# A three-block model on one core: the up products of the feed-forward stages by seven half-size products per pair of weight tiles

## The reference

```python
def sq_relu_mlp(h, w_up, w_down):          # first block, both layers, width 4096
    return jnp.square(jax.nn.relu(h @ w_up)) @ w_down
```

## Time and profile before

| | |
|---|---|
| median of 3 runs | 2861.84 us (2861.54 to 2865.23) |
| span of the profiled execution | 2860.9 us |
| TensorE busy | 98% of the span, granted clock 0.993 in the mean |
| VectorE, ScalarE, GpSimd busy | 52%, 35%, 48% |
| HBM | 94 GB/s over the span |

### The profile page before, as it was taken

The page is one execution under the profiler, slowest core; times in us unless marked ns, Lnnn a source line. Parts: engine busy times, 40 slices in busy tenths (PEclk is TensorE's granted clock), DMA queues, the critical chain, the costliest instruction groups (busy, mean ns, idle before and its releaser), DMA issues.

```text
span 2860.9 us, 43560 instructions
## 1 busy us (share of the span) xinstructions
PE 2799.9 (98%) x17428; PEld 2463.7 (86%) x17428; DVE 1479.0 (52%) x2439; ACT 1000.0 (35%) x1489; POOL 1376.9 (48%) x1748
## 2 busy tenths in 40 slices
PE   9989999999999999999899999999999999999999
PEld 7768888877788888998799999999989799999887
DVE  8955322267532227897644544233798745444241
ACT  4453222255422224443353322223443345322221
POOL 6426554555654556542225555456542225555554
PEclk9999999999999999999999999999999999999999
DMA  5103322222232224223324222222322243332322
GB/s 187 60 25 103 102 96 89 97 97 79 96 96 92 96 99 126 98 74 98 85 83 142 88 89 92 94 85 93 113 81 78 65 118 116 98 102 89 102 90 74
DMA packets 122630, 270.79 MB, mean 95 GB/s; under 512 B 22864, under 2 KB 57040, under 8 KB 122192
## 3 DMA queue, kind: packets, MB, share of 16 engines
q1 hardware_dynamic: 73104, 245.98, 26.0%
q10 hardware_dynamic: 49344, 22.19, 2.8%
HBM read 249.52 MB, written 18.61 MB: 94 GB/s over the span
## 4 chain that ended last, share of the span: by engine, by line
PE 42%; issue 29%; POOL 24%; DVE 4%; POOLq 0%; ACT 0%; DMA 0%; ACTq 0%; DVEq 0%
PE acc L666 33%; POOL w_lo L638 24%; PE acc L1078 2%; PE acc L1059 2%; PE aux L1059 2%; PE aux L1092 1%; DVE index_score L2706 1%; DVE best L2699 1%; PE acc L1286 0%; PE aux L969 0%; PE acc L1092 0%; PE acc L920 0%; PE aux L1278 0%; PE aux L951 0%; PE acc L1148 0%
## 5 line engine op out<-in xcount | busy, mean ns | idle before, releaser
L638 POOL TENSOR_TENSOR w_lo<-w_raw,w_hi 128x256 fp32r<-128x256 f32 x1744 | 1376.7, 821 | 1467.8 <-ACT w_hi L1320 1467.0
L666 PE MATMUL acc<-n_hi,w_hi 128*128 128x264 f32 (+1 forms) x2824 | 756.9, 323 | 2.3 <-DVE index_k L2398 1.3
L666 PE MATMUL acc<-n_lo,w_hi 128*128 128x264 f32 (+1 forms) x2824 | 748.0, 320 | 0.0
L666 PE MATMUL acc<-n_hi,w_lo 128*128 128x264 f32 (+1 forms) x2824 | 746.0, 319 | 0.0
L1320 ACT ACTIVATE w_hi<-w_raw 128x1024 fp32r<-128x1024 f32 (+1 forms) x436 | 454.1, 1043 | 615.2 <-PE acc L666 561.5
L666 PEld LDWEIGHTS acc<-n_hi,w_hi 128*128 128x128 f32 x2824 | 470.4, 188 | 59.8 <-issue 15.0
L666 PEld LDWEIGHTS acc<-n_lo,w_hi 128*128 128x128 f32 x2824 | 467.3, 188 | 40.9 <-issue 2.6
L666 PEld LDWEIGHTS acc<-n_hi,w_lo 128*128 128x128 f32 x2824 | 467.2, 188 | 38.3
L2214 DVE TENSOR_TENSOR x<-x,acc 128x512 f32<-128x512 f32 (+1 forms) x144 | 99.7, 692 | 562.6 <-PE acc L666 519.3
L666 PE MATMUL acc<-hidden_lo,w_hi 128*128 128x512 f32 (+1 forms) x1040 | 343.3, 358 | 0.0
L666 PE MATMUL acc<-hidden_hi,w_lo 128*128 128x512 f32 (+1 forms) x1040 | 342.7, 357 | 0.0
(11 more groups left out here) (484 smaller groups left out, 3750.0 us busy)
## 6 DMA issues: line engine op xcount, KB each, us to landing
w_raw<-in_stream SPq DMA_DIRECT2D x420, 512.0 KB, 3.5
unit_blocks<-unit_scratch ACTq DMA_DIRECT2D x26, 256.0 KB, 4.0
w_raw<-in_stream SPq DMA_DIRECT2D x16, 384.0 KB, 3.0
unit_scratch<-unit_staged ACTq DMA_DIRECT2D x20, 256.0 KB, 2.8
saved_x<-x SPq DMA_DIRECT2D x2, 2112.0 KB, 10.5
x<-saved_x SPq DMA_DIRECT2D x16, 264.0 KB, 2.7
saved_gates<-root ACTq DMA_DIRECT2D x12, 264.0 KB, 2.1
unit_scratch<-unit_staged ACTq DMA_DIRECT2D x1, 2560.0 KB, 13.4
```

Of the source, the lines that this page charges most:

```text
L638: i = pool.tensor_tensor(wl[:, slot, s], raw[:, slot, s], wh[:, slot, s].bitcast(F32), ALU.subtract)
L666: last = pe.matmul(o, w[:, p % W_SLOTS, P * b:P * b + P], r, start=(b == 0 and i == 0), stop=(b == n - 1 and i == 2))
```

## The change

The four feed-forward stages are reordered. The hidden tiles are cut into chunks of 4 (in a layer 3, 3, 4, 4, 4, 4). The first chunk is computed as before ("whole"). From then on a "pair" of pieces (in an mlp stage two up tiles, in a layer the gate and the value tile) is a 2x2 matrix of halves: two tiles by rows 0 to 511 and 512 to 1023, against the tokens' 2x2 matrix of row halves by token halves (256 or 264 tokens). Its eight half-size products are replaced by seven (Strassen's scheme in Winograd's form), named a11, s1, a12, s2, s4, s3, a22 in the order in which they run. Each is four blocks by three matmuls of 256 or 264 columns, into banks of `aux`. s1, s2, s4, s3 use sums of weight halves, which DVE makes from `w_raw` (s3 in place in `w_raw`), and sums of the normed tokens, made once per stage before the second whole tile is taken out. ACT copies three intermediate products out of PSUM (`keep_product`), DVE adds them to others (`pair_product`).

Pieces are split by half pieces ("ops"): the ring now has eight halves, and ACT and POOL split each of the seven factors (512 columns each) instead of the two pieces. Down pieces hold two output tiles of a chunk of 4. After a pair's first six products come the down pieces that are due (two in an mlp stage, one in a layer with chunks of 4), each of two ops, and only then a22. `freed` tells SP when a slot of `w_raw` may be loaded again: for the first piece of a pair when s3 has been split, for the second when a22 has. POOL's loop becomes straight code.

Per mlp stage there are 4 whole pieces, 14 pairs and 64 down ops; per layer 6 whole pieces, 19 pairs and 48 down ops. The cut diff:

```diff
+MLP_CHUNKS = [(n, n + 4) for n in range(0, FF // P, 4)]
+FFN_CHUNKS = [(0, 3), (3, 6)] + [(n, n + 4) for n in range(6, FT2, 4)]
+
+
+def chunks_of(stage):
+    return MLP_CHUNKS if stage.startswith("mlp") else FFN_CHUNKS
+
+
+def feed_steps(stage):
+
+    chunks, gated = chunks_of(stage), stage.startswith("layer")
+    order = [("whole", 0, n) for n in range((2 if gated else 1) * chunks[0][1])]
+    for e in range(1, len(chunks)):
+        n = (chunks[e][1] - chunks[e][0]) // (1 if gated else 2)
+        for i in range(n):
+            order.append(("pair", e, i))
+            order += [("down", e - 1, k) for k in range(4 * i // n, 4 * (i + 1) // n)]
+    return order + [("down", len(chunks) - 1, k) for k in range(4)]
...
+FACTORS = ("a11", "s1", "a12", "s2", "s4", "s3", "a22")
+SUMS = ("s1", "s2", "s4", "s3")
+LATER = 2
...
+    def freed(self, p):
+
+        found = [n + 1 for n, (kind, piece, _) in enumerate(self.ops) if piece == p or (piece == p - 1 and kind == "a22")]
+        paired = [n + 1 for n, (kind, piece, _) in enumerate(self.ops) if piece == p and kind == "s3"]
+        return paired[0] if paired else max(found)
...
-            sp.wait_ge(w_lo, p - RAW_SLOTS + 1)
+            sp.wait_ge(w_lo, order.freed(p - RAW_SLOTS))
...
-        with nc.Fori(0, pieces, W_SLOTS, engines=(mybir.EngineType.Pool,)) as p:
-            for slot in range(W_SLOTS):
-
-                pool.wait_ge(w_hi, p + slot + 1)
-                for part in range(4):
-                    s = slice(2 * P * part, 2 * P * part + 2 * P)
-                    i = pool.tensor_tensor(wl[:, slot, s], raw[:, slot, s], wh[:, slot, s].bitcast(F32), ALU.subtract)
-                i.then_inc(w_lo, 1)
-
+        for o, (kind, p, part) in enumerate(order.ops):
+            slot, at = order.half(o)
+            n = width_of(o)
+            source = weights_of(o)
+            pool.wait_ge(w_hi, o + 1)
+            for a in range(0, n, 2 * P):
+                z = min(a + 2 * P, n)
+                i = pool.tensor_tensor(wl[:, slot, at + a:at + z], source[:, a:z],
+                                       wh[:, slot, at + a:at + z].bitcast(F32), ALU.subtract)
+            i.then_inc(w_lo, 1)
...
+            def banded(o, bank, hi, lo, opens):
+
+                slot, at_ = order.half(o)
+                for b in range(KT // 2):
+                    for i, (w, v) in enumerate(((wh, hi), (wh, lo), (wl, hi))):
+                        mm = pe.matmul(aux[:, bank, 0:width], w[:, slot, at_ + P * b:at_ + P * b + P], v[:, b, :],
+                                       start=(opens and b == 0 and i == 0), stop=(b == KT // 2 - 1 and i == 2),
+                                       skip_group_check=True)
+                mm.then_inc(w_used, 1)
+
...
+                elif kind == "s2":
+                    if u == 0:
+                        pe.wait_ge(t_ready, sums + 2)
+                    pe.wait_ge(product_kept, kept + 3 * u + 1)
+                    banded(o, X_BANK[u % 2], th[:, 1, :, 0:width], tl[:, 1, :, 0:width], False)
...
+        def split_before(o):
+
+            while at["split"] < len(order.ops):
                 q = at["split"]
...
+                if order.turned[q] + (LATER if order.ops[q][0] in SUMS else 0) > o:
+                    return
+                split_one()
...
+            for o in feed["ops"][:-KT]:
+                kind, p, u = order.ops[o]
+                split_before(o)
+                if kind == "a11":
+                    pair, since = u, 0
+                if kind in ("a11", "s1", "s2"):
+                    keep_product(o, u, SEQ // 2)
+                if kind == "s1" and u:
+                    hidden_high(feed["whole"] + 2 * u - 1)
+                if kind == "down":
+                    since += 1
+                    if since == 2:
+                        hidden_high(feed["whole"] + 2 * pair)
...
+            if name == "s1":
+                for q in (p, p + 1):
+                    dve.wait_ge(landed[q % RAW_SLOTS], 16 * (q // RAW_SLOTS + 1))
+            if name != "s3" and at["split"][n]:
...
+            if name == "s1":
+                i = dve.tensor_tensor(s1, a21, a22, ALU.add)
+            elif name == "s2":
+                i = dve.tensor_tensor(s2, s1, a11, ALU.subtract)
+            elif name == "s4":
+                i = dve.tensor_tensor(s4, a12, s2, ALU.subtract)
+            else:
+                i = dve.tensor_tensor(a21, a21, a11, ALU.subtract)
+            i.then_inc(w_sum, c.made(w_sum))
+            at["sum"] = c.mine()
...
+            whole(0)
+            token_sums(stage, gains)
+            whole(1)
+            token_sum_low(stage, 0)
+            weight_sum_of(stage, 0, "s1")
+            token_sum_low(stage, 1)
+            weight_sum_of(stage, 0, "s2")
+            whole(2)
+            token_sum_low(stage, 2)
+            weight_sum_of(stage, 0, "s4")
+            token_sum_low(stage, 3)
+            weight_sum_of(stage, 0, "s3")
+            whole(3)
+            low()
+            if layer:
+                two_norms_ahead()
...
+                if kind == "a12":
+                    pair, since = u, 0
+                    pair_product(o, ub[:, 0, 0:width], Y_BANK, 0, width)
                     if waiting:
                         low()
...
+                elif kind == "s4":
+                    pair_product(o, ub[:, 0, width:SEQ], Z_BANK, 2, width)
+                    dve.wait_ge(*c.mine())
+                    scaled = step(dve.scalar_tensor_tensor(ub[:, 0, 0:SEQ], ub[:, 0, 0:SEQ], 0.0, scale[:, ROW], ALU.max, ALU.mult))
+                elif kind == "s3":
+                    pair_product(o, ub[:, 1, width:SEQ], X_BANK[u % 2], 1, width)
+                    half_out = c.mine()
+                    dve.wait_ge(*scaled)
+                    squared(feed["whole"] + 2 * u)
+                    weight_sum_of(stage, u + 1, "s1")
+                elif kind == "a22":
+                    dve.wait_ge(w_used, o + 1)
+                    dve.scalar_tensor_tensor(ub[:, 1, 0:width], aux[:, X_BANK[u % 2], 0:width], 0.0, scale[:, first],
+                                             ALU.max, ALU.mult).then_inc(pair_out, c.made(pair_out))
+                    lower = c.mine()
+                    dve.wait_ge(*half_out)
+                    upper = step(dve.scalar_tensor_tensor(ub[:, 1, width:SEQ], ub[:, 1, width:SEQ], 0.0, scale[:, second],
+                                                          ALU.max, ALU.mult))
+                    weight_sum_of(stage, u + 1, "s3")
+                    dve.wait_ge(*lower)
+                    dve.wait_ge(*upper)
+                    squared(feed["whole"] + 2 * u + 1)
+                    if u == feed["pairs"] - 1:
+                        low()
+                elif kind == "down":
+                    down(o, d, stage, SEQ)
+                    d, since = d + 1, since + 1
+                    if since == 1:
+                        weight_sum_of(stage, pair + 1, "s2")
+                    elif since == 2:
+                        weight_sum_of(stage, pair + 1, "s4")
+                        low()
...
+                elif kind == "s4":
+                    pair_product(o, ub[:, i % 2, HALF:T], Z_BANK, 2, HALF)
+                    dve.wait_ge(*c.mine())
+                    gate = step(dve.tensor_tensor(ub[:, i % 2, :], ub[:, i % 2, :], scale[:, :], ALU.mult))
+                    weight_sum_of(stage, u + 1, "s1")
+                    convolve(i, gate)
+                elif kind == "s3":
+                    pair_product(o, rt[:, HALF:T], X_BANK[u % 2], 1, HALF)
+                    half_out = c.mine()
+                    weight_sum_of(stage, u + 1, "s2")
+                elif kind == "a22":
...
+                    gated(i, rt[:, :], upper)
+                    weight_sum_of(stage, u + 1, "s3")
```

More of the change, by code:

```diff
@@ L1464, in mixer0 @@
                 job()
[L1465 removed]
+            act.wait_ge(mixer_landed, 16)
             slopes(0)
@@ new lines, in layer @@
+            whole = feed["whole"] // 2
+            for i in range(whole):
+                split_before(used(at["piece"]))
+                gate_silu(i)
+                if i == 1:
+                    token_sums_high(stage)
+                split_before(used(at["piece"] + 1))
+                at["piece"] += 2
+                hidden_high(i)
+            for o in feed["ops"][:-KT]:
+                kind, p, u = order.ops[o]
+                split_before(o)
+                if kind in ("a11", "s1", "s2"):
+                    keep_product(o, u, HALF)
+                if kind == "s1" and u:
+                    hidden_high(whole + u - 1)
+                if kind == "s3":
+                    gate_silu(whole + u)
@@ L1783, in by_head @@
+            hidden_high(whole + feed["pairs"] - 1)
+            c.next(pair_out, 4 * feed["pairs"])
+            at["piece"] = feed["end"]
+            if STAGES[-1] != stage:
+                last_downs(feed, T, lambda k: vec2_(l + 1, "norm_mix_2", k))
+            else:
```

(13 more changed lines are left out.)

756 lines of the change are left out of this document (525 added, 231 removed).

## The result

The changed kernel takes **2963.7 us** (median of 4 runs, 2963.4 to 2966.8) against 2861.7 before: ratio 1.0362, 95% interval 1.0348 to 1.0377. It is 102 us slower; 2962 was forecast.

The account below looks back on a forecast made before the run. TensorE was taken to bound the kernel before, POOL's pair cycles after the change. To 2861.8 us it added 65.2 (mlp), 12.7 (layer0) and 22.6 (layer1), together +100.5: 2962 us, range 2838 to 3015.

Parts of the forecast that it names:

- TensorE's saving and pace: In all four feed-forward stages, 256-column matmuls at 0.119 us each; net 80 us saved if TensorE stays the limit.
- The rival of the slow weight load: Narrow matmuls on TensorE paced by their weight load, 0.189 us each; about 3197 us; chance 0.02.
- The mlp loop: In mlp pair cycles, a loop outside TensorE from s1 to the next s1: 23.6 us against 22.2 before, +19.6 per stage.
- turns: POOL and DVE alternate at SBUF: each two-SBUF-input DVE instruction costs a working POOL 0.45 us; 3.8 per mlp cycle.
- landing: In mlp cycles, loading the next pair's second piece after a22's split, then DVE's sum, ACT's rounding and hand-overs: 5.0 us.
- the half: POOL's time to split half a piece, including a hand-over of about 0.04 us: 1.48 us.
- TensorE stays the bound: Rival for the pair cycles: POOL seldom disturbed, so the kernel gets faster; 2820 us, or 2841; chance 0.20.
- The layer's cycle: In the layers' pair cycles, POOL at 17.8 us exceeds TensorE's 16.2; 18.0 taken in layer0, 17.8 in layer1.
- second loop: In the layers, a chain from a22 through DVE, ACT and TensorE back to a22, as long as POOL's: 16.9 to 17.7 us.
- The late chains: Rival in the layers: DVE waits for s3's half before the convolution, cycle 17.9 to 19.6; 3027 us; chance 0.10.
- Starts and the chunk of three pairs: In the layers, 5 us per start; three-pair chunk 53.8 us on POOL, costing +0.9 in layer0 and +2.8 in layer1.
- mlp starts: At each mlp stage's start, ACT rounds s1, s2, s4, s3 late behind hidden tiles: 11.5 us per stage, bounds 0 and 15.

Follow-up runs that it names:

- number 1: Changed kernel with a22 placed behind the first down piece after its pair, not behind all of them, in all four stages: 2898.3 us, 1.0130.
- number 8: Changed kernel with a22 behind the first down piece, s2, s4, s3 rounded earlier at mlp starts, and a11's copy ahead of roundings in layers: 2887.1 us, 1.0102.
- number 10: Pairs in the mlp stages only, with a22 early and start sums rounded earlier; the layers' feed-forward networks as in the kernel before: 2851.0 us, 0.9964.
- number 7: Changed kernel; in layers ACT copies a11's product before the roundings and POOL makes only half of each factor's low part (rest stale): 2897.8 us, 1.0127.
- number 2: Changed kernel with four added DVE scratch instructions, two SBUF inputs each, per mlp pair ahead of the wait for the load: 3010.4 us, 1.0528.
- number 4: Changed kernel; at mlp starts ACT rounds s2 ahead of the third hidden tile and s4, s3 ahead of the fourth: 2960.6 us, 1.0356.
- number 5: Changed kernel; in the layers ACT copies a11's product out of PSUM before rounding s3 and two down halves: 2947.9 us, 1.0311.
- number 6: Changed kernel; in the layers POOL makes the low part of only the first 256 of each factor's 512 columns, others stale: 2902.1 us, 1.0151.

## Why the prediction was right, point by point

**TensorE's saving and pace: right.** 12 matmuls of 256 columns take 1.41 to 1.43 us (0.118 each; 0.119 forecast). In numbers 1, 8 and 10 the mlp cycle is 21.0 where 21.1 was worked out; number 7 shows 16.0 in layer0 and 15.8 in layer1 where it was 16.2 and 15.85. The rival of the slow weight load is out.

**The mlp loop: right in kind, 0.9 us a cycle too dear.** Forecast 14.8 (ten halves) + 3.8 (turns) + 5.0 (landing) = 23.6; measured 17.65 + 5.04 = 22.7. In the stretch shown POOL's 20 instructions follow each other every 0.695 us where nothing disturbs them, 13.9 in all; seven take about 1.2 and two about 1.0, which makes the other 3.7. The term that was mis-sized is the half, 1.48 us: it held a hand-over for each half, and in a run there is none, since ACT rounds ahead. That is 14 x 0.9 = 13 us per stage, of which 11 and 8 are left once the starts are counted; number 1 shows that the placing of a22 is the whole of the loss within the cycles.

**The turns: right in the pair cycles, wrong at the start of an mlp stage.** In the cycles they cost 3.7 us against 3.8 in mlp, and 0.38 each by number 2 against 0.45. At the start, six such instructions without a pause between them cost POOL 4.6 us, 0.77 each (number 4). The rival "TensorE stays the bound" fell with them in the layers: there turns are 17.3 - 18 x 0.695 = 4.8 us of a cycle (4.5 forecast), and without them POOL's 12.5 would be far under TensorE's 16.2. In mlp it took the landing and the turns together: with a22 early and all turns left in, TensorE is the bound again (number 1), and by the sum above the loop without its 3.7 us of turns would be 19.0, under TensorE's 21.0 too.

**The layer's cycle: right in kind, 0.6 too dear.** 18.0 and 17.8 forecast, 17.3 and 17.2 measured in the steady part, again by the hand-overs. The "second loop" over ACT and DVE that I gave as equally long is no bound there (number 5 shortened it and won 0.2 us); in pairs 4 to 7, where POOL has smaller halves, shortening it helps (number 5), and so does less work on POOL (number 6). The late chains (3027 us) did not come.

**Starts and the chunk of three pairs: wrong, and this is the step that failed.** The prediction said that in a layer "three pieces go per cycle, so the second piece's slot is freed [...] earlier, and the landing is hidden", and charged POOL alone for the chunk: 53.8 us. The third pair has two down pieces, so four pieces go in it, as in an mlp cycle, and the landing that I had found there stands open here too. The first three cycles took 69.9 us in layer0 and 68.5 in layer1, 16 and 15 more than the 53.8 charged, and the 5 us charged for a start do not cover that. By the prediction's own terms the three cycles would be 17.2, 17.2 and 19.5; measured were 25.4, 17.4 and 27.1 in layer0 and 23.8, 17.4 and 27.3 in layer1. So the landing in the third pair is 7.6 and 7.8 us of the miss, and the rest is the first cycle, that is the start. Number 1 takes 6.8 and 7.9 us of the three cycles away (the landing), and number 6, without that edit, 7.8 in layer0 (POOL's share, nearly all of it in the first two cycles). For layer0 the account against TensorE's own time (387.9 - 27.9 = 360.0) is: chunk of three pairs 21.4 us where 5.3 was forecast, the other 16 pairs 24 where 29 was, the first whole tiles 3.5 where 5 was, and some 4 for the end and the stretches at 1.2 GHz where 1 was: 53 in place of 40. What part of the first cycle's 25.4 us falls to DVE's token and weight sums, and what to ACT's order, was not separated.

**mlp starts: right in size, wrong in reason.** 11.5 us and 1.5 for the end were charged. In number 8, where all cycles are TensorE's own, mlp0 takes 353.4 us against 357.4 - 14 x 1.12 = 341.7: 11.7 for start and end together, after the 1.8 us that number 4 had won at the gap; in mlp1 it is 10.6. But ACT's order was given as the cause of the gap. Number 4 rounds s1 four us earlier and TensorE gets it 1.8 earlier: what holds it is POOL, kept out by DVE's run of two-input instructions, which the price of 0.45 a turn does not show.

**The sum** came out within 2 us of the median (104.1 between the profiled executions, 100.5 forecast) because the two errors have opposite signs: 19 us too much in mlp, 25 too little in the layers, -2 elsewhere. That they cancel is luck. Not luck are the sign of the change, the landing loop in mlp and POOL as the bound of the layers' steady cycle. The misses of the parts, 19 and 25 us, would each have stayed inside the range of 2838 to 3015.

## What to carry to other kernels

Where an operation is placed later to save a wait, ask which buffer it still holds, and who must load into it: here one product at the end of the order put 3.5 us of transfer and 1.5 us of chain into the loop of every mlp pair. That made the cycle 1.8 us longer than TensorE's own and cost 66 us in all by number 1, the layers' third pairs included, where the scheme saves 80 on TensorE. A ring with as many slots as a cycle uses pieces leaves slack only as far as a slot is freed early in the cycle: number 1 has the same ring and no wait in mlp. Check that count for every cycle, and for the odd one first. And trading TensorE's columns for work of VectorE and GpSimd pays only while their shared work stays below the shorter cycle: in mlp (11 halves in 21 us) it did, in the layers (9 halves and nine two-input instructions in 16) it did not.

## What the runs showed of the hardware that was not expected

**VectorE can keep GpSimd out for far longer than one instruction.** In number 4 an instruction of POOL that takes 0.70 us alone lasted 5.31 us, as long as six DVE instructions with two SBUF inputs followed each other every 0.60 us (1.14 for the wide ones). The same pattern, 5.31 and 5.32 us, stands at both mlp starts of number 10. In the pair cycles the two engines took turns instead (1.2 us at most), and at the start of layer0 POOL's longest instruction was 1.74; what decides between the two was not separated.

**Very short instructions of VectorE wait for GpSimd's turn.** In mlp0 of the changed kernel `lru_rates` works on 8 columns; from 270.2 to 271.5 us POOL is idle, from 271.51 on it works:

```profile
270.50 0.17 DVE L2545 TENSOR_TENSOR lru_rate<-lru_rate,vec 128x8 f32<-128x8 f32 x1
...
271.39 0.17 DVE L2532 TENSOR_TENSOR lru_rate<-lru_rate 128x8 f32<-128x8 f32 x1
271.59 0.68 DVE L2533 TENSOR_TENSOR lru_rate<-lru_rate 128x8 f32<-128x8 f32 x1
272.30 0.67 DVE L2534 TENSOR_SCALAR lru_rate<-lru_rate 128x8 f32<-128x8 f32 x1
273.00 4.81 DVE L2536 SCALAR_TENSOR_TENSOR lru_rate<-lru_rate 128x8 f32<-128x8 f32 x7
```
```profile
271.51 2.81 POOL L775 TENSOR_TENSOR w_lo<-weight_sum,w_hi 128x256 fp32r<-128x256 f32 x4 [1.28 <-ACT w_hi L1538]
274.27 9.07 POOL L775 TENSOR_TENSOR w_lo<-w_raw,w_hi 128x256 fp32r<-128x256 f32 x13
```

0.17 us becomes 0.66 to 0.69, in step with POOL's 0.695, while POOL itself is not slowed. L2534 is slowed as well, though it reads one tile only, so for these a second SBUF input is not the condition. Each operation waits for the one before it, and so falls in step with POOL: the nine from 271.59 to 277.81 take 6.2 us, where 0.21 apart they would take 1.9. And it costs time. In mlp0 of number 10 the chain ends at 282.4, and in DVE's order behind it stands L2712, which adds up a product that TensorE waits for ahead of a22:

```profile
282.44 0.75 DVE L2712 TENSOR_TENSOR unit_a<-aux,kept_product 128x256 f32<-128x256 f32 x2
...
284.40 0.36 PE L1048 MATMUL aux<-token_sum_hi,w_hi 128*128 128x256 f32 x1 [1.89 <-DVE unit_a L2712]
```

From its first a11 to the second TensorE takes 34.7 us in that stage, and 30.1 in mlp1, which has no such chain and no such gap.
